# GDN stage of a two-block kernel: clears moved on GpSimd, right sides moved on VectorE, modulation groups spread over three iterations

## The reference

```python
def gdn_chunked(q, k, v, log_a, beta, s0, with_output):
    ...
    dec = jnp.exp(jnp.where(incl, gam[..., :, None] - gam[..., None, :], -jnp.inf))
    kk = jnp.einsum('bhncd,bhnsd->bhncs', k, k)
    a_mat = jnp.where(strict, beta[..., :, None] * dec * kk, 0.0) + jnp.eye(GDN_CHUNK, dtype=jnp.float32)
    rhs = jnp.concatenate([beta[..., None] * v, (beta * jnp.exp(gam))[..., None] * k], axis=-1)
    uw = lax.linalg.triangular_solve(a_mat, rhs, left_side=True, lower=True, unit_diagonal=True)
    ...
    def step(s, inp):
        u_c, w_c, kd_c, gl_c = inp[:4]
        delta = u_c - jnp.einsum('bhcd,bhde->bhce', w_c, s)
        s_new = gl_c[..., None, None] * s + jnp.einsum('bhcd,bhce->bhde', kd_c, delta)
        if with_output:
            qd_c, p_c = inp[4], inp[5]
            o = jnp.einsum('bhcd,bhde->bhce', qd_c, s) + jnp.einsum('bhcs,bhse->bhce', p_c, delta)
            return s_new, o
        return s_new, None
```

## Time and profile before

| | |
|---|---|
| median of 3 runs | 2763.08 us (2761.68 to 2763.38) |
| the profiled execution | 2763.38 us, span from first to last instruction 2761.7 us |
| TensorE busy | 2634.1 us (95%) |
| VectorE / ScalarE / GpSimd busy | 1439.4 / 1017.3 / 257.3 us |
| GDN stage | from 512.7 us to about 872 us of the span |

### The profile page before, as it was taken

How to read it: one execution, slowest core, us unless ns; L and a number is a source line. 1 busy time by engine, 2 the same in 40 slices (tenths; PEclk the granted TensorE clock), 3 DMA queues, 4 the chain that set the end, 5 groups by cost and what they waited for, 6 DMA issues and landing times.

```text
span 2761.7 us, 46015 instructions
## 1 busy us (share of the span) xinstructions
PE 2634.1 (95%) x19718; PEld 2078.3 (75%) x19718; DVE 1439.4 (52%) x1954; ACT 1017.3 (37%) x1687; POOL 257.3 (9%) x208
## 2 busy tenths in 40 slices
PE   6989999899997999899999999999999999999998
PEld 4745688678886788778888777788888776788886
DVE  4565499456677433466653546453353446552442
ACT  3335576233333322333333436422223346321222
POOL 0220001223231000101101001100001001100001
PEclk8989999899999999999999999999999989999999
DMA  6100122240003232323222211223223211223321
GB/s 247 57 18 20 61 69 69 92 157 4 4 4 108 90 96 95 122 77 98 93 93 93 90 56 46 83 92 99 92 92 98 85 44 49 92 92 96 95 92 69
DMA packets 64714, 222.89 MB, mean 81 GB/s; under 512 B 7168, under 2 KB 7552, under 8 KB 64384
## 3 DMA queue, kind: packets, MB, share of 16 engines
q1 hardware_dynamic: 63360, 216.81, 24.0%
q10 hardware_dynamic: 1152, 3.15, 0.3%
HBM read 213.64 MB, written 6.29 MB: 80 GB/s over the span
## 4 chain that ended last, share of the span: by engine, by line
PE 62%; DVE 2%; issue 1%; ACT 0%; POOL 0%; POOLq 0%; ACTq 0%; DVEq 0%
PE ps L309 50%; PE ps L2416 6%; PE ps L319 2%; PE ps L2467 1%; PE ps L2497 1%; PE ps L2448 1%; PE ps L2470 1%; PE ps L2452 0%; PE ps L2485 0%; DVE src_lo_buf L2157 0%; DVE w_lo L287 0%; PE ps L2081 0%; DVE norm_sq_buf L517 0%; DVE diff_weight L2863 0%; DVE pool_csum L2888 0%
## 5 line engine op out<-in xcount | busy, mean ns | idle before, releaser
L287 DVE TENSOR_TENSOR w_lo<-ring,w_hi 128x1024 fp32r<-128x1024 f32 (+1 forms) x339 | 423.6, 1250 | 865.5 <-ACT w_hi L279 865.4
L279 ACT CAST w_hi<-ring 128x1024 fp32r<-128x1024 f32 (+1 forms) x339 | 352.8, 1041 | 958.5 <-PE ps L309 845.4
L309 PE MATMUL ps<-u_hi,w_hi 128*128 128x512 f32 x864 | 343.6, 398 | 9.1 <-DVE u_lo L504 9.1
L309 PE MATMUL ps<-u_hi,w_lo 128*128 128x512 f32 x864 | 343.5, 398 | 0.0
L309 PE MATMUL ps<-u_lo,w_hi 128*128 128x512 f32 x864 | 340.4, 394 | 0.0
L309 PE MATMUL ps<-mid_hi,w_lo 128*128 128x512 f32 x688 | 273.6, 398 | 0.0
L309 PE MATMUL ps<-mid_hi,w_hi 128*128 128x512 f32 x688 | 270.9, 394 | 0.0
L309 PE MATMUL ps<-mid_lo,w_hi 128*128 128x512 f32 x688 | 270.7, 393 | 0.0
L309 PEld LDWEIGHTS ps<-u_hi,w_hi 128*128 128x128 f32 x864 | 162.5, 188 | 51.2 <-issue 8.9
L309 PEld LDWEIGHTS ps<-u_lo,w_hi 128*128 128x128 f32 x864 | 162.6, 188 | 40.6 <-issue 0.5
L309 PEld LDWEIGHTS ps<-u_hi,w_lo 128*128 128x128 f32 x864 | 162.6, 188 | 39.6
(11 more groups left out here) (411 smaller groups left out, 4698.5 us busy)
## 6 DMA issues: line engine op xcount, KB each, us to landing
ring<-in_w_up SPq DMA_DIRECT2D x44, 512.0 KB, 3.5
ring<-in_w_in SPq DMA_DIRECT2D x42, 512.0 KB, 3.5
o_tok<-in_w_mod_rest SPq DMA_DIRECT2D x32, 512.0 KB, 4.7
ring<-in_w_merge SPq DMA_DIRECT2D x32, 512.0 KB, 3.5
ring<-in_w_mlp1a SPq DMA_DIRECT2D x32, 512.0 KB, 3.5
ring<-in_w_mlp2a SPq DMA_DIRECT2D x32, 512.0 KB, 3.5
ring<-in_w_mlp1b SPq DMA_DIRECT2D x32, 512.0 KB, 3.5
ring<-in_w_mlp2b SPq DMA_DIRECT2D x32, 512.0 KB, 3.5
```

The lines of the kernel that those rows point to most:

```text
L279: nc.scalar.copy(w_hi[:, slot, 0:width], ring[:, n % RING, 0:width]).then_inc(*hi_ok.one())
L287: nc.vector.tensor_tensor(w_lo[:, slot, 0:width], ring[:, n % RING, 0:width], as_f32(w_hi[:, slot, 0:width]), ALU.subtract).then_inc(*lo_o ...
L309: mm = nc.tensor.matmul(dst[:, a:b], w[wi][:, k * P:(k + 1) * P], src[xi][:, k0 + k, a:b], start=start and k == wi == xi == 0, stop=stop a ...
```

## The change

Three things. First, GpSimd makes `beta_decay` of all four groups of iteration 0 in its first piece, and the three clears in piece 1 get a wait for `dU1` of iteration 0, direction 0. Second, `right_side` of a moves from VectorE's piece 2 to piece 3, behind `one_off`, and that of b from piece 3 to piece 4, behind the level's operation and in front of `out_of_state`. Third, iteration 0 has ten groups of modulation instead of twelve (pieces 3 and 7 have none) and two new places take a group: piece 10 of iteration 1 in each direction. The waits that guard the PSUM banks follow.

```diff
-            rest_at = [(0, k, 1) for k in range(12)] + [(1, 4, 0), (1, 4, 1), (2, 4, 0), (2, 4, 1)]
+            rest_at = [(0, k, 1) for k in (0, 1, 2, 4, 5, 6, 8, 9, 10, 11)] + \
+                      [(1, 4, 0), (1, 10, 0), (1, 4, 1), (1, 10, 1), (2, 4, 0), (2, 4, 1)]
             REST_END = (2, 5, 1)
-            REST_0 = 12
+            REST_0 = 10
...
-                            if k == 0 and n < STEPS and not ahead(n):
+                            if k == 0 and n < STEPS and n > CS:
                                 beta_decay(n, a)
                                 beta_decay(n, b)
+                            elif k == n == d == 0:
+                                for g in range(G):
+                                    beta_decay(0, g)
...
                             elif k == 1 and n == d == 0:
+                                pool.wait_ge(*dU1.at(d_of(0, 0)))
                                 nc.gpsimd.memset(t64[:], 0.0).then_inc(*zero_ok.one())
...
-                                if t >= 0:
-                                    right_side(t, a)
                             elif k == 3:
                                 if prepare:
                                     one_off(n, d)
                                 if t >= 0:
-                                    right_side(t, b)
+                                    right_side(t, a)
                                 if t >= CS:
                                     out_of_state(t, a)
                             elif k in (4, 6, 8, 10):
                                 if prepare:
                                     level_y(n, (k - 4) // 2, d)
+                                if k == 4 and t >= 0:
+                                    right_side(t, b)
                                 if k == 4 and t >= CS:
                                     out_of_state(t, b)
...
-                                if (t, g) == (rest_at[j][0] - 1, rest_g(j)):
+                                if (t, 4, g) == (rest_at[j][0] - 1, rest_at[j][1], rest_g(j)):
                                     pe.wait_ge(*rows_ok.at(j + 1))
                                     pe.wait_ge(*mod_b.at(j - 1))
...
                                 pe.wait_ge(*dS.at(n_of(n - 2, g)))
+                                for j in range(REST_0, N_REST):
+                                    if (n, 10, g) == (rest_at[j][0] + 1, rest_at[j][1], rest_g(j)):
+                                        pe.wait_ge(*rows_ok.at(j + 1))
+                                        pe.wait_ge(*mod_b.at(j - 1))
...
+                            elif j < N_REST and rest_at[j][1] == 10:
+                                pe.wait_ge(*dS.at(n_of(rest_at[j][0] - 1, rest_g(j))))
                             else:
```

## The result

| | before | after |
|---|---|---|
| median of 5 runs | 2763.38 us (2761.68 to 2769.24) | 2784.72 us (2779.69 to 2796.19) |
| span of the profiled execution | 2761.7 us | 2783.1 us |
| GDN stage in it | 363.7 us | 380.1 us |
| everything behind the stage | 1885.3 us | 1890.0 us |

After to before is **1.0079, 95% interval 1.0058 to 1.0101**. That is above the forecast of 2755.3 us and above its range.

The account below looks back on a forecast made before the run. TensorE's own work was taken as the GDN stage's limit from 635 to 855 us, with stalls before that winnable. Terms summed to -7.75 us, forecasting 2755.3 us; own range 2752 to 2759, 8-in-10 range 2750.5 to 2763.5.

Parts of the forecast that it names:

- Part 1: GpSimd's clears go behind the first inverse level, so TensorE starts it at 525.2 instead of 528.90: 3.7 us earlier.
- Part 2, DMA waits: Moving two modulation groups out of iteration 0 lets the weight-transfer queue catch up before 578 us: -1.1 us.
- Instruction pauses: The 1.34 us gap near 578 us, late instructions, falls elsewhere with less traffic: -0.8 us, bounds 0 and -1.34.
- My last sentence: Forecast wrong if stage length changed where nothing was priced, above all iteration 1's start, where two extra groups stand.
- Part 2, clock at 580: TensorE's clock, 0.51 from 580 to 587 us, stays up once the gaps before it shrink: -3.0 us.
- The 0.96 us at 629: TensorE's gap before L1598 falls by most of the right side's time: -0.55 us; low clock behind it, -1.5.
- Part 3, waits: TensorE's turned v starts 0.9 us later in four halves, iterations 2 to 5: +3.6 us, bounds +1.2 and +4.8, or 0.
- The port: On VectorE, the second right side, with two SBUF inputs, waits for GpSimd's second L1189 of 1.04 us to end.
- the slower rival: Right side delays the 32-level in all eleven halves, 1.7 us each: +7.3 us in sum, 2770.4 us; chance 0.10.
- At the tail: At the stage's end the second right side no longer precedes the first L1343, for which TensorE waits: -0.7 us.
- The clock: Low-clock stretches in the stage from 580 us and behind 629 us go: -3.0 and -1.5 us.
- The clock does not care: Rival: both low-clock stretches stay or move, the instruction stall too, leaving -2.45 us, 2760.6 us; chance 0.22.

Follow-up runs that it names:

- e1: Kernel before with only GpSimd's four decay operations first and its three clears behind the first inverse level: -1.0 us, ratio 0.9978 to 1.0003.
- e2: Kernel before with only both right sides moved one piece later: +18.4 us, ratio 1.0050 to 1.0093.
- e7: Kernel before with both right sides in VectorE's piece 3, so only that of a moves: +17.9 us, ratio 1.0044 to 1.0104.
- g1: Kernel before with 128 small matmuls added ahead of TensorE's first level, shifting later instructions by 512: +1.9 us against before.
- h1: Kernel before with two extra VectorE transposes ahead of the second decayed scores in iteration 2, direction 0, making TensorE wait once: +8.0 us.
- f11: Kernel before with 40 small matmuls in TensorE's idle time ahead of the first level, shifting later instructions by 160: +13.4 us against before.
- f9: Kernel before with both right sides one piece later and GpSimd's second state scaling waiting for the second right side: +3.1 us against before.
- g3: Changed kernel with GpSimd's second state scaling made to wait for the second right side: +16.1 us against the kernel before.
- e3: Kernel before with only the modulation groups spread over three iterations, with their waits: +15.9 us, ratio 1.0034 to 1.0079.
- e5: Changed kernel without 28 of the 32 modulation weight transfers, same instructions, modulation wrong: +1.0 us against the kernel before.
- e4: Kernel before with the GpSimd reordering and the spread modulation groups, right sides unmoved: +6.7 us, ratio 1.0019 to 1.0059.
- h3: Changed kernel with 64 small matmuls ahead of the first level, shifting later instructions by 256: +18.1 us against the kernel before.

## Why the prediction was wrong, point by point

- **Part 1**: right in the trace: -3.7 us, first level at 525.25 against 525.2. The clears disturbed nothing.
- **Part 2, DMA waits**: right, -1.4 for -1.1. **Instruction pauses**: wrong in sign, +5.9 for -0.8. The step that failed: "it falls elsewhere and with less traffic beside it". There was not less traffic, only later traffic, and the earlier trace rows had already said that instructions under traffic can come 1.34 us late. Both my bounds were gains, 0 and -1.34; with a pause possible at every 256th instruction that meets transfers, the one above should have been a loss of several microseconds. Part of the +5.9 is chance: e1, e2, e7, g1 and h1 have a pause of 2.1 to 2.5 us at one and the same matmul of iteration 0, which the profile of the kernel before happens to have without a pause. My last sentence had the place (the start of iteration 1) but no price.
- **Part 2, clock at 580**: it rose to 0.76 there, but fell in other places. The 0.96 us at 629 went (0.40), the low clock behind it didn't, since a pause of 2.65 came three microseconds later.
- **Part 3, waits**: right. Four halves, waits of 0.93 and three of 1.53, less the pauses of before that went with them (0.24, and 0.10 + 0.19 + 0.18 in each later half): 0.7 + 3 x 1.06 = 3.9 us for 3.6. The port was right as well, 1.51 us for L1336 where 1.55 was worked out. In direction 0's halves nothing waited, as said; the slower rival's mechanism did not come here, but it is what e7 ran into. At the tail the 0.96 us went (-0.7 forecast).
- **The clock**: the term that decides, and the second step that failed. Forecast -4.5 us, measured +13.3. I took 1.5 us of gain for the removal of one wait of 0.96 us, by the slow stretch behind it, and then added four waits of 0.9 to 1.5 us and priced them at their own length. The same row should have priced both. "The clock does not care" was no cover for that, since it had no case in which the clock gets worse. With h1's 8 us for one wait the slower side would have held most of the chance.
- **Behind the stage**: forecast no change, measured +4.7 us, below. Its cause is open.

The direct terms thus sum to -1.3 - 1.4 = -2.7 us for a forecast of -2.45 (the rival in which clock and pause give nothing). The 24 us above that are the clock in the stage (13.3), instruction pauses (5.9) and 4.7 behind it. That the direct terms come out so close to their forecast is not luck, since the waits stand in the trace one by one; but they were the smaller part.

## What to carry to other kernels

Where TensorE is over 95% busy at the full clock, price each new wait of about a microsecond with the slow stretch that may follow it, here up to 20 us at half speed and 8 us of time (interval 3 to 10) for one wait of 1.23 us, and look in the profile of before for a wait of that length and what stands behind it. A background transfer is not free because nobody waits for it: with it spread over a longer time, TensorE stood still three times as long in the profile waiting for instructions (8.7 for 2.9 us), with no semaphore to show for it, only the late reads of its instructions on the DMA queue; and even an edit that adds matmuls only where TensorE was idle (f11) can cost 13 us by moving those pauses, so a control that shifts the program belongs beside any change of a few microseconds. An operation of VectorE with two SBUF inputs should be issued ahead of GpSimd's, not beside it; one wait on the GpSimd side (f9) took 15 of 18 us back with part 3 alone, and 5 of 21 in the changed kernel (g3).

## What the runs showed of the hardware that I had not expected

- An instruction pause can last 3.1 us, as in e3 on TensorE, while e5 without transfers has none over 0.53 us. The Trainium skill (Runtime: NRT & Kernel Launch, Instruction fetch mechanics) has the crossing of a 16 KiB boundary mostly hidden; the runs agree only for the kernels without transfers (1.7 and 2.2 us in the whole stage), and beside transfers the measurement decides. The longest pause, in e3:

```profile
593.59 0.61 PE L1599 MATMUL ps<-gdn_y,gdn_t 32*32 32x16 f32 x28 [3.08 <-issue]
```

- The kernel's own scatter, 2753 to 2777 us, goes with the clock: of the 131 runs of the kernel before beside the experiments, the fastest (2753.4 us) had a mean granted clock of 0.975 and the slowest (2777.0) one of 0.967, and over all of them 0.001 less goes with 2.0 us more.
- Behind the stage the large matmuls (L309) from about 950 to 1150 us ran at 216 matmuls in 50 us in the changed kernel and 220 in others, both at the full clock and with no pause; these are the changed kernel and e4:

```profile
1000.00:1050.00 50.00, 50.00 (x216) 40.51 (x215) 14.81 (x15) 11.57 (x15) 0.00 (x0) 1.00 0.30 95
```

```profile
1000.00:1050.00 50.00, 50.00 (x221) 41.00 (x220) 15.39 (x16) 11.42 (x13) 0.00 (x0) 1.00 0.30 95
```

The three profiles of kernels with all three parts and their transfers (after, g3, h3) have it and take 1889.5 to 1890.0 us behind the stage; the others take 1881.8 to 1886.4. The cause is open.
